# Two transformer blocks in float32 on one core: GpSimd splits the plain unit of an up pair before the last parts of its Strassen unit

## The reference

```python
def _squared_relu_mlp(h, w1, w2):
    a = jax.nn.relu(h @ w1)
    return (a * a) @ w2

def first_block(x, ...):          # HGRN2 mixer
    ...
        x = x + mix
        x = x + _squared_relu_mlp(_rmsnorm(x, norm_mlp[layer]), mlp_w1[layer], mlp_w2[layer])
    return _rmsnorm(x, norm_final)

def second_block(x, ...):         # convolution and retention mixer
        h = h + hybrid_mixer(rms_norm(h, norm1_g), w_in, conv_w, conv_norm_g, ret_norm_g, w_out)
        h = h + sq_relu_mlp(rms_norm(h, norm2_g), w_up, w_down)
    return rms_norm(h, final_norm_g)
```

## Time and profile before

| What | us |
|---|---|
| Median of 3 runs | 2380.12 |
| Lowest and highest | 2380.11, 2380.45 |
| The profiled execution's own time | 2377.08 |
| Its span | 2374.5 |
| Mean granted TensorE clock | 0.997 |
| TensorE busy | 2331.4 (98%) |
| VectorE busy | 1499.9 (63%) |
| GpSimd busy | 1068.4 (45%) |
| ScalarE busy | 724.5 (31%) |

### The profile page before, as it was taken

One profiled execution on the slowest core, in us unless ns is written; L12 is line 12 of the kernel. 1 busy time (PEld: TensorE's weight loads), 2 busy tenths in 40 slices (PEclk: granted clock), 3 DMA queues, 4 the chain that ended last, 5 costly groups with the idle time before them and its releaser, 6 DMA issues.

```text
span 2374.5 us, 31836 instructions
## 1 busy us (share of the span) xinstructions
PE 2331.4 (98%) x11044; PEld 1939.2 (82%) x11044; DVE 1499.9 (63%) x2090; ACT 724.5 (31%) x1175; POOL 1068.4 (45%) x1186
## 2 busy tenths in 40 slices
PE   9999999999999999999999999999999999999998
PEld 6888888888787778778888888888877877787886
DVE  6666667756567666765566656454666676667434
ACT  4233333423433432333330002003343333323311
POOL 4322232345456555645443324453554565555432
PEclk9999999999999999999999999999999999999999
DMA  4110101031111111111111111111111111111112
GB/s 151 36 36 27 36 26 36 27 107 62 45 54 54 51 54 53 53 44 54 54 52 64 36 45 36 54 36 54 38 54 52 53 53 44 60 55 45 49 58 80
DMA packets 37526, 123.33 MB, mean 52 GB/s; under 512 B 4800, under 2 KB 5952, under 8 KB 37440
## 3 DMA queue, kind: packets, MB, share of 16 engines
q1 hardware_dynamic: 36432, 120.54, 16.0%
q10 hardware_dynamic: 1008, 1.62, 0.2%
HBM read 117.95 MB, written 4.19 MB: 51 GB/s over the span
## 4 chain that ended last, share of the span: by engine, by line
PE 82%; POOL 7%; issue 7%; DVE 2%; DVEq 1%; DMA 0%; SPq 0%; ACT 0%; POOLq 0%
PE prod_ps L563 13%; PE prod_ps L565 13%; PE prod_ps L564 13%; PE side_ps L822 4%; PE side_ps L821 4%; PE side_ps L820 4%; POOL w_lo L454 4%; PE prod_ps L822 4%; PE prod_ps L821 4%; PE prod_ps L820 4%; PE prod_ps L905 3%; PE prod_ps L906 3%; PE prod_ps L907 3%; PE side_ps L700 2%; PE side_ps L616 2%
## 5 line engine op out<-in xcount | busy, mean ns | idle before, releaser
L563 PE MATMUL prod_ps<-operand_hi,w_hi 128*128 128x512 f32 x1464 | 584.0, 399 | 2.9 <-DVE hgrn_v_t L1150 1.6
L565 PE MATMUL prod_ps<-operand_hi,w_lo 128*128 128x512 f32 x1464 | 572.6, 391 | 0.0
L564 PE MATMUL prod_ps<-operand_lo,w_hi 128*128 128x512 f32 x1464 | 571.4, 390 | 0.0
L454 POOL TENSOR_TENSOR w_lo<-w_raw,w_hi 128x256 fp32r<-128x256 f32 x472 | 470.5, 1027 | 9.4
L450 POOL CAST w_hi<-w_raw 128x1024 fp32r<-128x1024 f32 x118 | 125.9, 1067 | 733.8 <-PE prod_ps L565 680.2
L484 POOL TENSOR_TENSOR w_lo<-w_raw,w_hi 128x256 fp32r<-128x256 f32 x160 | 144.0, 918 | 454.6 <-ACT w_hi L2172 454.6
L563 PEld LDWEIGHTS prod_ps<-operand_hi,w_hi 128*128 128x128 f32 x1464 | 275.9, 188 | 61.1 <-issue 3.3
L565 PEld LDWEIGHTS prod_ps<-operand_hi,w_lo 128*128 128x128 f32 x1464 | 275.5, 188 | 59.1
L564 PEld LDWEIGHTS prod_ps<-operand_lo,w_hi 128*128 128x128 f32 x1464 | 276.1, 189 | 53.4
L905 PE MATMUL prod_ps<-operand_hi,w_hi 128*128 128x512 f32 x384 | 151.7, 395 | 22.5 <-POOL w_lo L454 22.5
L906 PE MATMUL prod_ps<-operand_lo,w_hi 128*128 128x512 f32 x384 | 150.5, 392 | 0.0
(11 more groups left out here) (304 smaller groups left out, 4655.2 us busy)
## 6 DMA issues: line engine op xcount, KB each, us to landing
w_raw<-stream SPq DMA_DIRECT2D x202, 512.0 KB, 3.5
x_in<-x_t SPq DMA_DIRECT2D x16, 256.0 KB, 5.6
x_res<-x_t SPq DMA_DIRECT2D x8, 512.0 KB, 4.4
out_t<-x_res SPq DMA_DIRECT2D x16, 256.0 KB, 2.1
w_raw<-stream SPq DMA_DIRECT2D x8, 128.0 KB, 4.8
masks_f<-masks SPq DMA_DIRECT2D x1, 896.0 KB, 7.4
ret_rows<-head_rows ACTq DMA_DIRECT2D x1, 512.0 KB, 3.7
ret_cos<-rope ACTq DMA_DIRECT2D x1, 512.0 KB, 4.6
```

The costliest lines, as they stand in the source:

```text
L454: low = nc.gpsimd.tensor_tensor(w_lo[:, slot, ks], w_raw[:, slot, ks], w_hi[:, slot, ks].bitcast(F32), ALU.subtract)
L563: nc.tensor.matmul(into, w_h, a_h, start=(k == 0), stop=False)
L564: nc.tensor.matmul(into, w_h, a_l, start=False, stop=False)
L565: last = nc.tensor.matmul(into, w_l, a_h, start=False, stop=(k == KT - 1))
```

## The change

`split_pair` gets a parameter `between`, a function that it calls after the S2 low. For up pairs this is the splitting of the plain unit. GpSimd's order in an up pair was A11 and A12, S1, S2, S3 and S4, A22, plain cast, four plain lows; now it is A11 and A12, S1, S2, plain cast, four plain lows, S3 and S4, A22. The plain unit's last low no longer counts up `w_split` but a new semaphore `upper_split`, for which TensorE waits ahead of `upper(b_w)`; the A22 low counts up `w_split` by two. `high_made` is counted for the pair before the plain unit. TensorE's order is the same as before. Down pairs and all other units are unchanged.

```diff
+        upper_split = sem("upper_split")
...
-            def split_unit(u, slot):
+            def split_unit(u, slot, done=None):
...
-                low.then_inc(w_split, 1)
+                low.then_inc(w_split if done is None else done, 1)
...
-            def split_pair(u, slot, q):
+            def split_pair(u, slot, q, between=None):
...
                 low(w_lo[:, slot, 6:8], s12[slot][:, 2:4], w_hi[:, slot, 6:8], 3).then_inc(w_parts, 1)
+                if between is not None:
+                    pool.sem_inc(high_made, 1)
+                    between()
                 for ks in (slice(0, 2), slice(2, 4)):
                     part = low(s34_lo[slot][:, ks], s34[slot][:, ks], more_hi[slot][:, ks], 3)
                 part.then_inc(w_parts, 1)
-                low(a22_lo[slot][:], w_raw[:, slot, 6:8], more_hi[slot][:, 4:6], 4).then_inc(w_split, 1)
-                pool.sem_inc(high_made, 1)
+                low(a22_lo[slot][:], w_raw[:, slot, 6:8], more_hi[slot][:, 4:6], 4).then_inc(
+                    w_split, 1 if between is None else 2)
+                if between is None:
+                    pool.sem_inc(high_made, 1)
...
                 def up_pair(u, q):
-                    split_pair(u, 0, q)
-                    split_unit(u + 1, 1)
+                    split_pair(u, 0, q, lambda: split_unit(u + 1, 1, upper_split))
...
-                    pe.wait_ge(w_split, at(g, 8, u + 2))
+                    pe.wait_ge(upper_split, at(g, 2, first_up + r + 1))
                     upper(b_w, 0, 0, False, start).then_inc(up_prod, 1)
```

## The result

| What | us |
|---|---|
| Before, median of 4 runs | 2380.11 (2379.65 to 2380.45) |
| Changed, median of 4 runs | 2453.64 (2450.55 to 2455.17) |
| Ratio | 1.0307, 95% interval 1.029 to 1.0325 |
| Changed, profiled execution | 2455.17, span 2452.6, mean granted clock 0.98 |

The kernel is slower by 73.5 us, or 3.1%. The forecast was 2445, with a range of 2408 to 2472.

What follows compares the result with a forecast made beforehand. TensorE, busy 98% of the span, was taken to bound the kernel. Stalls of 46.5 us plus 18.8 of low clock on the profiled 2377.08 gave 2442.4; 3.0 for the median gave 2445 us, range 2408 to 2472.

Steps and rivals of the forecast that it cites:

- The order of demands: In up pairs TensorE wants S4 ahead of `upper(b_w)`, so the change hastens what is needed second by delaying the first.
- Near pairs: Near pair of each group, 12 in all: S4 stalls 4.83 us, the 1.87 at `upper(b_w)` goes; 35.5 us added.
- (a): Near pair: the plain cast can start 0.34 us after A11, 0.9 sooner than before, after GpSimd idles 1.1 us.
- (c): Near pair, cost of a low: 0.70 us for the first, 1.65 each for five beside VectorE's 1024-wide instructions.
- Far pairs: The 12 far pairs: S4's low just fits; 0.1 us each for a late weight load, 1.2 us in all.
- First pairs of a block: First pair of each block, two in all: a stall of 1.9 us at S4 with none before; 3.8 us.
- Second pairs: Second pair of each block, two in all: a stall of 2.7 us at S4, less 0.28 waited before; 4.8 us.
- Last two pairs: Last two pairs of each block, four in all: S4's lows 0.3 us late, 1.2 us in all.
- The sum of the stalls: All up pairs: the added stalls of TensorE sum to 46.5 us.
- The loads: Next Strassen unit's load into slot 0 starts later at no cost; cover of 3 to 5 us is left.
- The clock: Behind near-pair stalls TensorE works at the lower clock: 20.5 us less 1.7 paid before, 18.8 us added.
- I take one such stretch for each of the 12: Each near-pair stall is followed by one low-clock stretch of 3.42 us, costing 1.7 us; 20.5 us for the 12.

Runs made afterwards that it cites:

- e5: The changed kernel with TensorE taking `upper(b_w)` ahead of S4 in the near pairs of the groups; 2392.35 us, 1.005 of the kernel before.
- e1: The changed kernel with the S3 and S4 lows back ahead of the plain unit, only A22 behind it; 2368.74 us, 0.9956 of the kernel before.
- e3: The changed kernel with the A22 low moved ahead of the plain unit, S3 and S4 still behind it; 2453.13 us, 1.0312 of the kernel before.
- e4: The changed kernel with two of the plain unit's four lows left out in the groups' near pairs; 2385.61 us, 1.0018 of the kernel before.
- e2: The changed kernel with 21 extra TensorE matmuls ahead of the wait for S4's lows in the groups' near pairs; 2427.07 us, 1.0203 of the kernel before.
- e7: The changed kernel with 9 extra TensorE matmuls ahead of the wait for S4's lows in the groups' near pairs; 2441.76 us, 1.026 of the kernel before.
- e8: The kernel before, GpSimd's order untouched, with TensorE taking S3 ahead of `upper(b_w)` in the groups' near pairs; 2364.58 us, 0.9934 of the kernel before.

## Why the prediction was right, step by step

- **The order of demands.** That S4 stands ahead of `upper(b_w)` decided the sign. e5 shows it directly, and e1 and e3 show that S3 and S4, not A22, carry the cost.
- **Near pairs.** Forecast: cast 0.34 us after A11, S4 at 10.46 us after A11, a stall of 4.83 us, 35.5 us more. Measured: 0.34, 10.69, 4.93 to 4.99 us, 37.2 us more. The terms (a) and (c) hold: GpSimd idled 1.12 us, and e4 measured 1.67 us a low against the 1.65 used.
- **Far pairs.** Forecast 0.1 us each, measured 0.14 to 0.17 in nine of them, 0.38 in the first and nothing in the last of each block. **First pairs of a block:** forecast 1.9, measured 1.74. **Second pairs:** forecast 2.7, measured 2.05; the unit's four lows took 3.81 us where I had kept the 4.77 of before, since they started later and one of them met a long VectorE instruction instead of two, and S3 and S4 took 2.39 where I had allowed 1.9. **Last two pairs:** forecast 0.3, measured as a delay of S4 from 5.44 to 5.71 us after A11.
- **The sum of the stalls.** Forecast 46.5 us, of which 44.1 for pairs with a wait that the profile lists; measured 44.2 by these waits. e2, without the clock's part in the near pairs, lies 46.6 us above the kernel before on its chip (2380.52). That this agrees to 0.1 us is in part luck: the 46.6 also holds the low clock behind the second pairs' stalls where it occurs, some 3.4 us in e2's profiled execution, which the forecast put at nothing, and the kernel before is a median of executions that reach from 2377.05 to 2382.85.
- **The loads.** The later loads cost nothing, as worked out; the median landing was 3.6 us, and no wait for a landing stood in the up pairs.
- **The clock.** This term was mis-sized: 20.5 us forecast for the near stalls, before the 1.7 already paid is taken off, and 26.6 measured by e2. The step that failed is "I take one such stretch for each of the 12", with 3.42 us a stretch. Each near stall did have its stretch, but nine of the 12 lasted 6.8 us, of which 3.8 to 6.2 fell on work. The difference of 6.1 us is most of the 8.6 us between 2445 and 2453.6. The stalls of 2.05 us in the second pairs had a stretch too in the profiled execution, which the forecast did not count.
- The sentence of the Trainium skill (TensorE: Matmul & The Clock Gate, HAM oscillation) that a pause recurring in a loop pays each turn agrees with the trace of the changed kernel: 12 of 12. For shorter pauses in the same loop the traces show it less: 10 of 12 at 2.9 to 3.0 us (e7), one of 12 at 1.87 (before). By eleven of the 12 rows before, which would have made it 0, I would have been 27 us short.

## What to carry to other kernels

Before a producer's order is changed for the sake of the wait that the profile lists, list all that its consumer wants around that wait, in the consumer's order, with the time at which each is wanted: here the item moved back was wanted 1.4 us sooner than the one moved forward. If the wait is for one item of several, look first whether the consumer can do another of its items meanwhile (e8). And a longer stall of TensorE is dearer than its length: 4.98 us in place of 1.87 cost 3.1 us by itself and 2.2 us more by the clock.

## What the runs showed of the hardware

- How often the clock fell went with the length of a single idle. In the near pairs, 12 each: 1.65 us (e4) no stretch of low clock, 1.87 (before) one, 2.9 to 3.0 (e7) ten, 4.98 (changed) twelve. e5 has 2.0 us of idle in each near pair, in two pieces of 1.6 and 0.4, and none. One execution was profiled of each, and of the kernel before it was one of the shortest: executions of it beside the experiments reach from 2377.05 us at a mean granted clock of 0.997 to 2382.85 at 0.994. The longer ones had more time at the lower level; where it fell their results do not show, so one in 12 may be too few for a typical execution. Stalls of 1.74 us at the first pairs had none in any version. Those of 2.05 us at the second pairs had one at both pairs in the changed kernel, e2, e3 and e4, and at neither in e5 and e7.
- A stretch of low clock at these stalls lasted 3.4 or 6.8 us, also with TensorE fully busy in it, so a stall of 3 us could be followed by 6 us at half speed, as in e7.
- A GpSimd subtraction of 128x256 took 0.70 us alone and 1.67 beside VectorE's two-input instructions of 128x1024, which themselves took mostly 1.5 to 1.8 instead of 1.22. A small part of a gain in start time was then given back: in e1 the cast started 0.55 us after A11 instead of 1.25, and the four lows took 6.79 us where they had taken 6.62.
